# First feed-forwards: gate and up products of steps three to eleven all by Strassen's scheme

## The chip, the cores and the metric

One core of one Trainium2 chip runs the whole program. The time is that of one execution on the device in microseconds (us). The engines are named as in the profile: PE is TensorE (matmuls), DVE is VectorE, ACT is ScalarE, POOL is GpSimd, SP is SyncE, which issues the DMA loads.

## What is computed

A residual stream x of 512 tokens by 1024 features (float32) goes through two stacks of two layers. Each layer of the first stack is a feed-forward, a token mixing and a second feed-forward; each layer of the second is a mixing and a feed-forward with a causal convolution. The change touches the four feed-forwards of the first stack ("first feed-forwards"), cut to what matters:

```python
def rmsnorm(x, g):                       # x / sqrt(mean(x * x) + eps) * g
def swiglu(h, w_gate, w_up, w_down):     # silu(h @ w_gate) * (h @ w_up), then @ w_down
...
for l in range(DEPTH):                   # DEPTH 2, D_MODEL 1024, D_FF 2816
    f = swiglu(rmsnorm(x, ffn1_pre_g[l]), ffn1_w_gate[l], ffn1_w_up[l], ffn1_w_down[l])
    x = x + FFN_RESIDUAL_WEIGHT * rmsnorm(f, ffn1_post_g[l])
    m = token_mixing(...)
    x = x + rmsnorm(m, mix_post_g[l])
    f = swiglu(rmsnorm(x, ffn2_pre_g[l]), ffn2_w_gate[l], ffn2_w_up[l], ffn2_w_down[l])
    x = x + FFN_RESIDUAL_WEIGHT * rmsnorm(f, ffn2_post_g[l])
```

## The kernel before

**Numbers.** Float32 products are made of three matmuls on rounded halves: every weight and activation is split into a high part (a rounding copy by ScalarE) and a low part (the rest, a subtraction by VectorE), and TensorE adds high x high, high x low and low x high into one PSUM bank (`part_mm`, lines 698 to 700, and `tile_mm`, 647 to 649).

**Steps and granules.** The gate and up products of a feed-forward have eleven steps (0 to 10 in the code, one to eleven in words). A step makes 256 of the 2816 hidden columns and has four granules of 512 weight rows by 256 columns (512 KB): q = 0, 1 for w_gate into banks 0 to 3, q = 2, 3 for w_up into banks 4 to 7. A plain granule (`pe_up_granule`) is 8 tiles of 3 matmuls with 512 moving columns, so 24. A Strassen granule (`pe_strassen`) works on the 2 x 2 block form of the product in the Winograd variant: seven products in place of eight for each pair of row blocks, so 2 x 7 x 3 = 42 matmuls with 256 moving columns. It needs four sums of weight blocks (`sums_split`, tile wsum, then sumhi and sumlo), four sums of activation blocks (`t_sums`, `t_hi`, `t_lo`), and seven partial results that are put together behind it (`combine`).

**Which steps.** Steps one and two are plain. In the loop over steps three to ten (`FIRST` to `LAST` - 1) the gate granules are plain and the up granules Strassen. Step eleven is plain. Behind it come the w_down products (`pe_out`), in four column pairs of six granules.

**Order.** Each engine has its order written out by hand; semaphores tie them. Tiles raw, whi, wlo, sumhi and sumlo have two slots, q % 2. SP loads the raw weights of a granule when the low part of the granule two before is made (`load_raw`). ScalarE makes the high part when that granule's matmuls are over (`split_hi`, line 632). VectorE makes the sums (1361 to 1366), the low part of the weights (639) and, behind ScalarE's copy of the sums (1150), their low part (1369). TensorE waits for both low parts. VectorE waits for a result of its own by a semaphore (`ch.wait()`).

**VectorE's turn of the loop before** is: sums-and-split block of granule (i, 3); hidden product of the step before (1495), one hidden low part (1396); gate times r into S (1448), which frees banks 0 to 3; plain low parts of (i + 1, 0) and (i + 1, 1); `combine` of the up results (1384 to 1391), release of banks 4 to 7, two products with r (1461); block of (i + 1, 2). r is the inverse root of the mean square of x. ScalarE's turn has the high parts, the sums' copies, one hidden high part (1155) and two silus (1176).

## Time and profile before

| | us |
|---|---|
| median of two runs (3360.22 and 3362.19) | 3361.2 |
| the profiled execution, its span (the page gives no other time of it; the median is 1.7 above) | 3359.5 |
| TensorE busy | 3304.6 |
| VectorE busy | 2065.5 |
| ScalarE busy | 1504.9 |

The span runs from the first to the last instruction. Busy shares are averages over stages that have different limits, so stretches are read one by one. In a timeline row the first number is the start in us from the span's start and the second the duration; where a row stands for several instructions (x2), the duration is that of all. Durations of consecutive instructions of one engine overlap a little, so the distance from start to start is what one costs its queue. The first feed-forward runs from about 25 to 380 us of the span, its step three from 65.3.

### The profile page before, as it was taken

The numbers are of one execution on the slowest core, as the hardware profiler recorded it, in microseconds if no ns is written. First come the engines' busy times: TensorE is split into PE (matmuls) and PEld (weight loads), VectorE is DVE, ScalarE is ACT, GpSimd is POOL, SyncE is SP. The second block draws the span as 40 slices with busy tenths as digits, with TensorE's granted clock in tenths as the row PEclk, the third lists the DMA queues.
The fourth block names the chain that finished last, engine by engine and source line by source line (L and its number), as shares of the span: only waits on it lengthen the run. The fifth ranks groups of instructions, "written<-read, shape, count | busy, mean of one in ns | idle before, by whom it ended". The sixth has DMA issues, their size and how long they took to land.

```text
span 3359.5 us, 56027 instructions
## 1 busy us (share of the span) xinstructions
PE 3304.6 (98%) x22342; PEld 2941.2 (88%) x22342; DVE 2065.5 (61%) x2942; ACT 1504.9 (45%) x2508; POOL 289.8 (9%) x157
## 2 busy tenths in 40 slices
PE   8999999999999999999999999999999999999999
PEld 7887876788889888876788889889999998899998
DVE  6882556678627882556678726746665277476643
ACT  5342445543335342445553334565443254754432
POOL 1000022100000000022100001210000022100000
PEclk9999999999999999999999999999999999999999
DMA  4343321233333332321233332212223322122222
GB/s 120 100 125 102 106 57 57 70 91 98 97 98 88 100 99 92 105 59 55 70 89 99 93 102 76 57 47 78 93 87 96 102 68 55 57 82 91 90 88 88
DMA packets 330747, 287.62 MB, mean 86 GB/s; under 512 B 9697, under 2 KB 326201, under 8 KB 330581
## 3 DMA queue, kind: packets, MB, share of 16 engines
q1 hardware_dynamic: 330117, 284.17, 28.2%
q8 instruction: 121, 1.98, 0.3%
q10 hardware_dynamic: 464, 1.10, 0.1%
q14 instruction: 45, 0.37, 0.0%
HBM read 283.10 MB, written 5.27 MB: 86 GB/s over the span
## 4 chain that ended last, share of the span: by engine, by line
PE 90%; DVE 5%; ACT 3%; DMA 1%; issue 1%; ACTq 0%; SPq 0%; DVEq 0%
PE ps L647 18%; PE ps L648 18%; PE ps L649 18%; PE ps L698 6%; PE ps L700 6%; PE ps L699 6%; PE ps L753 2%; PE ps L2113 2%; PE ps L2115 2%; PE ps L2114 2%; PE ps L1698 1%; PE ps L757 1%; PE ps L1737 1%; PE ps L1722 1%; PE ps L2163 1%
## 5 line engine op out<-in xcount | busy, mean ns | idle before, releaser
L639 DVE TENSOR_TENSOR wlo<-raw,whi 128x1024 fp32r<-128x1024 f32 (+1 forms) x412 | 495.2, 1202 | 753.0 <-ACT whi L632 750.0
L632 ACT ACTIVATE whi<-raw 128x1024 fp32r<-128x1024 f32 (+1 forms) x493 | 511.6, 1040 | 946.7 <-PE ps L649 790.4
L647 PE MATMUL ps<-xhi,whi 128*128 128x512 f32 (+2 forms) x2576 | 864.5, 336 | 2.0 <-DVE wlo L639 2.0
L648 PE MATMUL ps<-xlo,whi 128*128 128x512 f32 (+2 forms) x2576 | 853.1, 331 | 0.0
L649 PE MATMUL ps<-xhi,wlo 128*128 128x512 f32 (+2 forms) x2576 | 850.6, 330 | 0.0
L647 PEld LDWEIGHTS ps<-xhi,whi 128*128 128x128 f32 x2576 | 485.9, 189 | 65.0 <-issue 17.5
L649 PEld LDWEIGHTS ps<-xhi,wlo 128*128 128x128 f32 x2576 | 484.5, 188 | 47.8
L648 PEld LDWEIGHTS ps<-xlo,whi 128*128 128x128 f32 x2576 | 485.6, 188 | 42.0 <-issue 0.5
L647 PE MATMUL ps<-hhi,whi 128*128 128x512 f32 (+2 forms) x1056 | 359.0, 340 | 0.7 <-issue 0.7
L648 PE MATMUL ps<-hlo,whi 128*128 128x512 f32 (+2 forms) x1056 | 358.1, 339 | 0.0
L649 PE MATMUL ps<-hhi,wlo 128*128 128x512 f32 (+2 forms) x1056 | 357.7, 339 | 0.0
L832 POOL TENSOR_TENSOR S<-S 128x512 f32<-128x512 f32 (+5 forms) x58 | 79.6, 1372 | 2236.1 <-ACT S L859 2184.2
L639 POOL TENSOR_TENSOR wlo<-raw,whi 128x1024 fp32r<-128x1024 f32 (+1 forms) x81 | 203.9, 2518 | 739.8 <-ACT whi L632 739.8
L647 PEld LDWEIGHTS ps<-hhi,whi 128*128 128x128 f32 x1056 | 198.9, 188 | 25.7 <-issue 2.5
L649 PEld LDWEIGHTS ps<-hhi,wlo 128*128 128x128 f32 x1056 | 198.5, 188 | 24.4
L648 PEld LDWEIGHTS ps<-hlo,whi 128*128 128x128 f32 x1056 | 198.9, 188 | 22.8
L700 PE MATMUL ps<-xhi,wlo 128*128 128x256 f32 (+2 forms) x544 | 153.0, 281 | 0.0
L1176 ACT ACTIVATE S<-S 128x512 f32<-128x512 f32 (+2 forms) x132 | 82.0, 635 | 156.2 <-DVE S L1448 116.5
L2113 PE MATMUL ps<-xhi,whi 128*128 128x264 f32 x480 | 145.5, 303 | 2.0 <-DVE m_vt L2513 1.1
L1433 DVE SCALAR_TENSOR_TENSOR S<-S,par 128x528 f32<-128x528 f32 (+1 forms) x176 | 126.3, 759 | 23.2 <-ACT S L1142 17.2
L698 PE MATMUL ps<-xhi,whi 128*128 128x256 f32 (+2 forms) x480 | 139.2, 290 | 0.0
L2114 PE MATMUL ps<-xlo,whi 128*128 128x264 f32 x480 | 137.7, 287 | 0.0
(322 smaller groups left out, 6714.9 us busy)
## 6 DMA issues: line engine op xcount, KB each, us to landing
raw<-in_ffn_w_up_dram SPq DMA_DIRECT2D x176, 512.0 KB, 3.7
raw<-in_ffn_w_down_dram SPq DMA_DIRECT2D x120, 512.0 KB, 3.5
raw<-in_w_in_dram SPq DMA_DIRECT2D x94, 512.0 KB, 3.8
raw<-in_ffn_w_gate_dram SPq DMA_DIRECT2D x88, 512.0 KB, 3.8
raw<-in_w_out_dram SPq DMA_DIRECT2D x32, 512.0 KB, 3.4
raw<-in_ffn_w_down_dram SPq DMA_DIRECT2D x24, 256.0 KB, 2.8
tbias_scratch<-rev_scratch SPq DMA_DIRECT2D x1, 3072.0 KB
y<-tbias_scratch SPq DMA_DIRECT2D x6, 512.0 KB, 4.7
```

Of the source, the lines that this page charges most:

```text
L632: act.activation(into[:, 0:n], raw[slot][:, 0:n], ACT.Copy).then_inc(b.s.weights_hi, 1)
L639: eng.tensor_tensor(lo[:, 0:n], raw[slot][:, 0:n], hi[:, 0:n].bitcast(F32), ALU.subtract).then_inc(b.s.weights_split, 1)
L647: pe.matmul(o, wh, hi[:, t0:t0 + w], start=first, stop=False)
L648: pe.matmul(o, wh, lo[:, t0:t0 + w], start=False, stop=False)
L649: ins = pe.matmul(o, wl, hi[:, t0:t0 + w], start=False, stop=last)
L698: pe.matmul(o, wh, hi, start=first, stop=False)
L699: pe.matmul(o, wh, lo, start=False, stop=False)
L700: return pe.matmul(o, wl, hi, start=False, stop=last)
L1176: act.activation(S[2 + o][:, 0:b.T], S[2 + o][:, 0:b.T], ACT.Silu).then_inc(b.s.silu_done, 1)
L1433: ins = dve.scalar_tensor_tensor(out=c_, in0=S[o][:, k:k + b.T], scalar=tap(l, k, 2 * i + o, up), in1=c_, op0=ALU.mult, op1=ALU.add)
L2113: pe.matmul(o, wh, xhi[:, t, t0:t0 + w], start=(t == 0), stop=False)
L2114: pe.matmul(o, wh, xlo[:, t, t0:t0 + w], start=False, stop=False)
```

## The change

- **TensorE**: the loop runs over steps three to eleven (9 turns), and all four granules of a step are Strassen granules. The gate's partial results use banks 0 to 3 and the up results' banks 4 to 7 in the same layout. Signs are arranged differently: the first hidden half of a step comes out negative and is turned back in `silu` and in the hidden splits.
- **VectorE**: four sums-and-split blocks a step. A block has three sums in place of four (one 128x512, two 128x256); the low part of the weights has 768 of 1024 columns, since one block of the four isn't used by itself. `combine` runs for gate and up; its first copy goes to ScalarE (`corner`). Gate times r is one 128x1024 operation, and so is the hidden product. The up results aren't multiplied with r. The hidden low parts of steps two to eleven leave the loop and stand behind it, between the first w_down splits.
- **ScalarE**: high parts of 768 columns, a copy of the sums with each, a corner copy for gate and up. The hidden high parts leave the loop, too.
- **Norm**: since the up results lack r, the w_down result is larger by 1 / r. The norm behind it takes that out, but for eps, so a tile ye with eps / r^2 in 128 shares is made by ScalarE beside the norm of x (`act_pre_norm`) and added by POOL to the sum of squares (`pool_y`), and the logarithm takes no bias there.

The core of the diff:

```diff
-STRASSEN_GRAN = 2 * (LAST - FIRST)
+ROUNDS = LAST - FIRST
+STRASSEN_GRAN = 4 * ROUNDS + 4
+COMBINED = 2 * ROUNDS + 2
 EARLY = UP_ITERS - 1
...
+            if KIND[g] == "F1":
+                act.activation(ye[:, t0:t0 + w], ps[:, sum_bank(g, f"pre {h}"), 0:w], ACT.Copy,
+                               bias=EPS * EPS * D / P, scale=EPS / P).then_inc(e.eps_made, 1)
...
+            if KIND[g] == "F1":
+                pool.wait_ge(e.eps_made, 2 * KIND[:g + 1].count("F1"))
+                pool.wait_ge(e.y_summed, done)
+                add(acc[:, 0:b.T], ye[:, 0:b.T])
...
+                        (0, 0, True, True, w(a, 1), xs(2 * kp, 0)),
+                        (1, 1, True, False, w(a, 3), xs(2 * kp + 1, 0)),
+                        (3, 0, True, False, w(a, 2), ts(3, kp)),
+                        (3, 1, False, True, ws(a, 3), xs(2 * kp + 1, 1)),
+                        (2, 0, True, False, ws(a, 0), ts(2, kp)),
+                        (1, 0, False, True, ws(a, 2), ts(1, kp)),
+                        (2, 1, False, True, ws(a, 1), ts(0, kp))):
+                    ins = part_mm(pe, ps[:, b0 + bank, h * hw:h * hw + hw], *wt, *mv,
+                                  s2 == 0 and a == 0 and first, s2 == 1 and a == 1 and last)
...
-                with pe.Fori(FIRST, LAST) as i:
+                with pe.Fori(0, ROUNDS + 1) as j:
                     for q in range(4):
-                        (pe_up_granule if q < 2 else pe_strassen)(pe, b, l, f, i, q)
-                for q in range(4):
-                    pe_up_granule(pe, b, l, f, LAST, q)
+                        pe_strassen(pe, b, l, f, FIRST + j, q, 4 * j + q + 1)
             pe.wait_ge(b.s.hidden_free, f.ev(l) + 2 * UP_ITERS - 1 + CR)
...
+            def blocks_hi(i, q, count):
+
+                act.wait_ge(b.s.weights_landed[q % 2], 16 * (f.gb2(l) + 2 * i + q // 2) + 16)
+                act.wait_ge(b.s.granules_done, gb + 4 * i + q + 1)
+                act.activation(blocks(whi[q % 2]), blocks(raw[q % 2]), ACT.Copy).then_inc(b.s.weights_hi, 1)
+                sums_hi(count, q)
+
+            def corner(i, up):
+
+
+                act.wait_ge(b.s.granules_done, gb + 4 * i + 2 * up + 2 + CR)
+                act.wait_ge(b.s.hidden_free, f.ev(l) + 2 * i + up + CR)
+                act.activation(S[0][:, SEQ // 2:SEQ], ps[:, 4 * up, 0:SEQ // 2], ACT.Copy).then_inc(b.s.corner_out, 1)
...
-                hi_split(2, 0)
+                blocks_hi(FIRST, 0, 1)
                 t_hi(2, 3)
-                hi_split(2, 1)
+                blocks_hi(FIRST, 1, 2)
                 if g == 0:
                     act_constants(act)
...
+                with act.Fori(0, ROUNDS) as j:
+                    i = FIRST + j
+                    corner(i, 0)
+                    blocks_hi(i, 3, 4 * j + 4)
+                    silu(i, True)
+                    blocks_hi(i + 1, 0, 4 * j + 5)
+                    corner(i, 1)
+                    blocks_hi(i + 1, 1, 4 * j + 6)
+                    blocks_hi(i + 1, 2, 4 * j + 7)
+                corner(LAST, 0)
+                blocks_hi(LAST, 3, STRASSEN_GRAN)
+                silu(LAST, True)
+                for k in range(2, BESIDE_LAST):
                     hidden_hi(k)
-                hi_split(LAST, 2)
-                for k in range(LAST + 6, 2 * LAST):
+                hi_split(LAST + 1, 0)
+                corner(LAST, 1)
+                hi_split(LAST + 1, 1)
+                for k in range(BESIDE_LAST, 16):
                     hidden_hi(k)
-                hi_split(LAST, 3)
-                silu(LAST)
-                hi_split(LAST + 1, 0)
...
+                v = raw[q % 2][:, :].rearrange("p (a x c) -> p a x c", a=2, x=4)
+                w = wsum[:, :].rearrange("p (a j c) -> p a j c", a=2, j=4)
                 dve.wait_ge(b.s.weights_landed[q % 2], 16 * (f.gb2(l) + 2 * i + q // 2) + 16)
-                if q == 3:
-                    dve.wait_ge(b.s.sums_split, count - 1)
-                elif not isinstance(i, int):
-                    dve.wait_ge(b.s.sums_split, count - 1)
-                ch(dve.tensor_tensor(s4[:, 0, :, :], a21, a22, ALU.add))
-                ch(dve.tensor_tensor(s4[:, 2, :, :], a11, a21, ALU.subtract))
+                dve.wait_ge(b.s.sums_split, STRASSEN_GRAN * n + count - 1)
+                ch(dve.tensor_tensor(w[:, :, 0:2, :], v[:, :, 1:3, :], v[:, :, 0:1, :].to_broadcast([P, 2, 2, P]),
+                                     ALU.add))
                 ch.wait()
-                ch(dve.tensor_tensor(s4[:, 1, :, :], s4[:, 0, :, :], a11, ALU.subtract))
+                ch(dve.tensor_tensor(w[:, :, 2, :], w[:, :, 1, :], v[:, :, 1, :], ALU.add))
                 ch.wait()
-                dve.tensor_tensor(s4[:, 3, :, :], a12, s4[:, 1, :, :], ALU.subtract).then_inc(b.s.sums_made, 1)
-                lo_split(i, q)
-                dve.wait_ge(b.s.sums_hi, count)
+                dve.tensor_tensor(w[:, :, 3, :], w[:, :, 2, :], v[:, :, 3, :], ALU.add).then_inc(b.s.sums_made, 1)
+                dve.wait_ge(b.s.weights_hi, gb + 4 * i + q + 1)
+                dve.tensor_tensor(blocks(wlo[q % 2]), blocks(raw[q % 2]), blocks(whi[q % 2]).bitcast(F32),
+                                  ALU.subtract).then_inc(b.s.weights_split, 1)
+                dve.wait_ge(b.s.sums_hi, STRASSEN_GRAN * n + count)
                 dve.tensor_tensor(sumlo[q % 2][:, :], wsum[:, :], sumhi[q % 2][:, :].bitcast(F32),
                                   ALU.subtract).then_inc(b.s.sums_split, 1)
 
-            def combine():
+            def combine(count, up):
...
+                dve.wait_ge(b.s.corner_out, COMBINED * n + count)
+                ch(dve.tensor_tensor(SS[:, 0:d + 2:d + 1, 0:hw], both(1),
+                                     p1.unsqueeze(1).to_broadcast([P, 2, hw]), ALU.add))
                 ch.wait()
-                ch(dve.tensor_tensor(SS[:, 0:5:4, 0:hw], both(5), p1.unsqueeze(1).to_broadcast([P, 2, hw]), ALU.add))
+                ch(dve.tensor_tensor(u, both(2), v2.unsqueeze(1).to_broadcast([P, 2, hw]), ALU.add))
                 ch.wait()
-                ch(dve.tensor_tensor(u, both(6), S[0][:, 0:hw].unsqueeze(1).to_broadcast([P, 2, hw]), ALU.add))
+                ch(dve.tensor_tensor(cross, both(3), u, ALU.add))
+                ch(dve.tensor_tensor(S[d][:, hw:SEQ], ps[:, b0 + 2, hw:SEQ], u[:, 0, :], ALU.add))
                 ch.wait()
-                ch(dve.tensor_tensor(cross, both(7), u, ALU.add))
-                ch(dve.tensor_tensor(S[5][:, hw:2 * hw], ps[:, 6, 0:hw], u[:, 1, :], ALU.add))
-                ch.wait()
 
             def hidden_lo(k):
...
+                two = SS[:, 2:4, 0:SEQ]
+                src = ps[:, 0:4:2, :]
+                if combined is not None:
+                    combine(combined, 0)
+                    src = two
+                dve.tensor_tensor(two, src, r[:, 0:SEQ].unsqueeze(1).to_broadcast([P, 2, SEQ]),
+                                  ALU.mult).then_inc(b.s.gate_in, 2)
                 dve.wait_ge(b.s.gate_in, f.hb(l) + 2 * i + 2)
                 dve.sem_inc(b.s.hidden_free, 1)
...
+            def hidden(i):
+
+                dve.wait_ge(b.s.silu_done, f.hb(l) + 2 * i + 2)
+                dve.tensor_tensor(hf[:, bass.ds(2 * i, 2), 0:SEQ], SS[:, 4:6, 0:SEQ], SS[:, 2:4, 0:SEQ],
+                                  ALU.mult).then_inc(b.s.hidden_done, 2)
...
+            gate(1)
+            t_sums()
+            sums_split(FIRST, 0, 1)
+            t_lo()
+            sums_split(FIRST, 1, 2)
+            plain_up(1)
+            sums_split(FIRST, 2, 3)
+            if g == 0:
...
+                sums_split(i, 3, 4 * j + 4)
                 dve.wait_ge(b.s.hidden_done, f.hb(l) + 2 * i)
-                gate(i)
-
-            start, stop, per = (1, UP_ITERS, 6) if b.conv else (FIRST, LAST - 1, 13)
-            with dve.Fori(start, stop) as i:
-                base, n0 = ch.base, ch.n
-                ch.base = base + (i - start) * per
-                if b.conv:
-                    lo_split(i, 3)
-                    gate(i)
-                else:
-                    step(i)
-                lo_split(i + 1, 0)
-                lo_split(i + 1, 1)
-                up(i)
+                gate(i, 2 * j + 1)
+                sums_split(i + 1, 0, 4 * j + 5)
+                sums_split(i + 1, 1, 4 * j + 6)
+                up(i, 2 * j + 2)
+                sums_split(i + 1, 2, 4 * j + 7)
+                hidden(i)
                 assert ch.n == n0 + per, ch.n - n0
-            ch.base, ch.n = base, n0 + per * (stop - start)
-            if not b.conv:
-                step(LAST - 1)
-                lo_split(LAST, 0)
-                lo_split(LAST, 1)
-                up(LAST - 1)
-                hidden(LAST - 1)
-                for k in range(LAST, LAST + 4):
-                    hidden_lo(k)
-                lo_split(LAST, 2)
-                for k in range(LAST + 4, 2 * LAST - 2):
-                    hidden_lo(k)
-                lo_split(LAST, 3)
-                dve.wait_ge(b.s.hidden_done, f.hb(l) + 2 * LAST)
-                gate(LAST)
-                for k in range(2 * LAST - 2, 2 * LAST):
-                    hidden_lo(k)
-                lo_split(LAST + 1, 0)
-                lo_split(LAST + 1, 1)
-                up(LAST)
-            dve_out(dve, b, g, gb + UP_GRAN, DOWN_Q, ch, 3)
+            ch.base, ch.n = base, n0 + per * ROUNDS
+            sums_split(LAST, 3, STRASSEN_GRAN)
+            dve.wait_ge(b.s.hidden_done, f.hb(l) + 2 * LAST)
+            gate(LAST, COMBINED - 1)
+            for k in range(2, BESIDE_LAST):
+                hidden_lo(k)
...
```

## Rows read from the trace of the kernel before

**Rows 1.** The page: busy shares, the chain, the loads of w_up.
```profile
PE 3304.6 (98%) x22342; PEld 2941.2 (88%) x22342; DVE 2065.5 (61%) x2942; ACT 1504.9 (45%) x2508; POOL 289.8 (9%) x157
...
PE 90%; DVE 5%; ACT 3%; DMA 1%; issue 1%; ACTq 0%; SPq 0%; DVEq 0%
...
raw<-in_ffn_w_up_dram SPq DMA_DIRECT2D x176, 512.0 KB, 3.7
```

**Rows 2.** Stretches: width, busy us (count) of TensorE, loads, VectorE, ScalarE, POOL; clock, DMA, GB/s.
```profile
86.25:97.60 11.35, 11.35 (x50) 9.08 (x49) 9.47 (x16) 3.19 (x3) 0.00 (x0) 1.00 0.34 96
76.29:86.25 9.96, 9.96 (x85) 9.91 (x83) 7.75 (x11) 4.85 (x6) 0.00 (x0) 1.00 0.26 83
97.61:118.93 21.32, 21.32 (x134) 18.95 (x134) 17.43 (x27) 8.04 (x10) 0.00 (x0) 1.00 0.35 98
54.20:65.30 11.10, 11.10 (x50) 9.00 (x49) 9.95 (x11) 7.26 (x8) 0.00 (x0) 1.00 0.27 81
...
65.30:259.10 193.80, 192.56 (x1153) 169.04 (x1152) 157.45 (x236) 77.78 (x97) 1.37 (x3) 1.00 0.38 114
```

**Rows 3.** VectorE in order of time: start, us, line, operation, idle before.
```profile
110.46 0.69 DVE L1386 TENSOR_TENSOR S<-ps,S 128x512 f32<-128x512 f32 x1
111.18 0.69 DVE L1388 TENSOR_TENSOR S<-ps,S 128x512 f32<-128x512 f32 x1
...
113.08 1.30 DVE L1461 TENSOR_TENSOR S<-S,r 128x512 f32<-128x512 f32 x2 [0.15 <-DVE S L1391]
114.62 0.42 DVE L1361 TENSOR_TENSOR wsum<-raw 128x256 f32<-128x256 f32 x1 [0.23 <-DVE S L1461]
114.96 0.42 DVE L1362 TENSOR_TENSOR wsum<-raw 128x256 f32<-128x256 f32 x1
115.41 0.42 DVE L1364 TENSOR_TENSOR wsum<-wsum,raw 128x256 f32<-128x256 f32 x1
115.87 0.42 DVE L1366 TENSOR_TENSOR wsum<-raw,wsum 128x256 f32<-128x256 f32 x1
...
117.42 1.23 DVE L1369 TENSOR_TENSOR sumlo<-wsum,sumhi 128x1024 fp32r<-128x1024 f32 x1
118.68 0.42 DVE L1361 TENSOR_TENSOR wsum<-raw 128x256 f32<-128x256 f32 x1
```

**Rows 4.** One group of one shape: count, busy us, mean ns, idle before.
```profile
L1950 DVE TENSOR_TENSOR m_w<-m_w,m_scan 128x768 f32<-128x768 f32 x6 | 5.7, 958 | 0.2
```

**Rows 5.** ScalarE in order of time.
```profile
103.84 1.23 ACT L1176 ACTIVATE S<-S 128x512 f32<-128x512 f32 x2 [3.18 <-DVE S L1448]
104.98 1.04 ACT L632 ACTIVATE whi<-raw 128x1024 fp32r<-128x1024 f32 x1
...
116.33 1.06 ACT L1150 ACTIVATE sumhi<-wsum 128x1024 fp32r<-128x1024 f32 x1 [1.94 <-DVE wsum L1366]
...
236.40 3.22 ACT L1155 ACTIVATE hhi<-hf 128x512 fp32r<-128x512 f32 x6
```

**Rows 6.** VectorE ahead of the loop.
```profile
56.55 1.28 DVE L1448 TENSOR_TENSOR S<-ps,r 128x512 f32<-128x512 f32 x2
57.98 1.23 DVE L1408 TENSOR_TENSOR tsum<-hf 128x1024 f32<-128x1024 f32 x1 [0.15 <-DVE S L1448]
...
62.66 1.22 DVE L639 TENSOR_TENSOR wlo<-raw,whi 128x1024 fp32r<-128x1024 f32 x1
```

**Rows 7.** TensorE's first product of w_down, in order of time.
```profile
259.10 0.47 PE L647 MATMUL ps<-hhi,whi 128*128 128x512 f32 x1 [0.73 <-issue]
```

**Rows 8.** Stretches at and after short stands of TensorE, columns as in rows 2.
```profile
3345.40:3347.20 1.80, 0.01 (x1) 0.05 (x1) 0.85 (x2) 1.39 (x4) 0.00 (x0) 1.00 0.00 0
3347.40:3351.30 3.90, 3.90 (x20) 3.63 (x19) 2.38 (x4) 2.73 (x6) 0.00 (x0) 0.56 0.10 42
...
2235.50:2248.40 12.90, 12.90 (x56) 10.65 (x54) 1.69 (x2) 4.54 (x12) 2.36 (x1) 0.50 0.12 41
1585.20:1587.00 1.80, 0.12 (x2) 0.13 (x2) 0.94 (x2) 1.39 (x3) 1.31 (x1) 1.00 0.00 0
```

More of the change, by code:

```diff
@@ L1501, in dve_ffn @@
                     ch(dve.memset(S[o][:, 0:2], 0.0))
+                gate(0)
+                lo_split(1, 1)
+                conv_up(0)
+                with dve.Fori(1, UP_ITERS) as i:
+                    base, n0 = ch.base, ch.n
+                    ch.base = base + (i - 1) * 6
+                    lo_split(i, 3)
+                    gate(i)
+                    lo_split(i + 1, 0)
+                    lo_split(i + 1, 1)
+                    conv_up(i)
+                    assert ch.n == n0 + 6, ch.n - n0
@@ new lines, in dve_ffn @@
+            ch.base, ch.n = base, n0 + per * ROUNDS
[4 more added lines that the diff above has]
+                hidden_lo(k)
+            lo_split(LAST + 1, 0)
+            lo_split(LAST + 1, 1)
+            up(LAST, COMBINED)
+            hidden(LAST)
+            for k in range(BESIDE_LAST, 11):
+                hidden_lo(k)
+            lo_split(LAST + 1, 2)
@@ L1557, in dve_out @@
+            for k in range(11, 18):
+                hidden_lo(k)
+            lo_split(LAST + 1, 3)
+            for k in range(18, KF):
+                hidden_lo(k)
+            dve_out(dve, b, g, gb + UP_GRAN, DOWN_Q, ch, 4)
         def dve_out(dve, b, g, gb, qs, ch, first=2):
```

212 lines of the change are left out of this document (95 added, 117 removed).

## The prediction

> **What bounds the kernel now.** I read the page first: TensorE is busy 98% of the span, and the chain that ended last lies on it for 90% [rows 1]. That names the bound of the whole, not of the stage that is changed, so the stretch windows come next. In step three of the first feed-forward its two Strassen granules take 9.96 us and the two plain ones after them 11.35; the next whole step takes 21.32, with TensorE busy in all of it and VectorE busy for 17.43 [rows 2]. The reader is to see two things: a pair of plain granules costs 1.4 us more than a Strassen pair, of which the loop's turn is part (the pair 54.20 to 65.30, outside the loop, takes 11.10); and VectorE already has only 3.9 us to spare of 21.3. So matmuls bound these steps today, and the question is whether they still do.
>
> **What TensorE saves.** Twenty granules of each first feed-forward turn from plain to Strassen: the gates of steps three to eleven (18) and the up products of step eleven (2). That is ten pairs at 11.10 - 9.96 = 1.14, or 11.4 us for each of four feed-forwards, about 46 us in all. A step's matmuls then take 2 x 9.96 = 19.9, with the loop's turn (about 0.2) 20.15. This is all the change can give: 1.4%.
>
> **What VectorE has to do for a step.** I walk its queue by distances from start to start, since they hold the overlap and the waits. One sums-and-split block, from the rows of today's block [rows 3]:
> - The first sum, now 128x512 and with a wait behind it: 0.73, as 110.46 to 111.18.
> - The second sum, 128x256 with a wait: 0.45, as 114.96 to 115.41.
> - From the start of the last sum to the low part of the sums: 1.55 today (115.87 to 117.42). Between them lies the low part of the weights, which shrinks from 1024 to 768 columns: a 128x768 operation takes 958 ns [rows 4], 1024 columns 1.23 us. I give nothing for that. The sums' low part needs ScalarE's copy of them, which starts at 116.33, when the last sum ends, and takes 1.06 [rows 5]: 117.39, and VectorE goes on at 117.42. The copy ends this wait already now; 0.42 + 1.06 and two hand-overs remain 1.55.
> - The low part of the sums: 1.26 ahead of another block (117.42 to 118.68); 1.15 ahead of an operation that doesn't wait for it, the 0.11 being what a wait adds (0.45 against the 0.34 of 114.62 to 114.96).
>
> That is 3.88 for a block, or 3.99. Today a step has two of these blocks (4.06) and two bare splits; the new one has four blocks, three at 3.88 and one at 3.99: 15.6. The combination from its second operation on took 110.46 to 113.08, so 2.62, and is now needed twice; that of the gate has no release of a bank behind it (2.52), but the 128x1024 product with r and its wait and release (1.15 + 0.23, the latter from 56.55 to 57.98 less two products at 0.60 [rows 6]; 0.60 as the third part of the combination, 0.61). The hidden product as one operation: 1.15. Behind the gate ScalarE does two silus (1.14 [rows 5]) before the high part of the next weights, under 1.04, which comes about 0.2 after VectorE's three sums (1.5) and its turn from the gate. Sum: 15.6 + 2.6 + 2.5 + 1.4 + 1.15 + 0.2 = **23.5 us a step**, against 20.15 of matmuls and 21.32 now. The hidden splits that leave the loop (0.6 a step) and the products of the up results with r are taken off in this.
>
> Does any of the waits hide it? In VectorE's order the gate's combination needs granule two of its step, which ended some 5 us before, and the up combination granule four, which ended about 6 us before. A raw buffer is freed at least 7.7 us before it is read again (low part 1.2, a block 3.9, the up combination 2.6), and a load of 512 KB lands in 3.7 [rows 1]. So nothing stretches VectorE's 23.5, and nothing shortens it: TensorE stands about 3.0 us before the first gate granule of each step and 0.5 elsewhere.
>
> **The ends of the loop.** Step three's gates now need the low parts of the x sums too. VectorE gets to its block for the first granule at 62.66, where the split stood [rows 6], ends it at 66.5, and the four low parts at 1.14 take it to 71.1. The plain gates started at 65.3 [rows 2], so TensorE stands 5.8 us. Then the second block (75.0), the products of step two (76.4), the third block (80.3), the fourth, held 0.5 by ScalarE's corner copy, which waits for the second granule until 81.2 (84.8). Eight periods of 23.5 follow: step eleven's last block ends at 272.8. Its last granule takes 5.0, but the first w_down weights come behind ScalarE's silus (until +5.0), six high parts at 0.53 (8.1), the high part of the weights, 1.04 (9.2), and VectorE's low part, 1.2 (10.4) [rows 5, 3]. w_down's products start at 283.3; today at 259.1 [rows 7]. **+24.2 us.** The hidden low parts that follow keep ahead: the last of them, near 299, is wanted at 283.3 + 20 x 1.39 = 311, with 1.39 as six products of 0.232 (11.10 / 48 [rows 2]). Four stages of one code and one size make 97; ScalarE's and VectorE's constants, 4 us of work in the first stage alone, now stand in the way there and cost about 1. Together 98.
>
> What is costed at nothing: the added copy of the mean square (two of 128x256 on ScalarE, each under the 0.53 of a 128x512 copy [rows 5], ahead of the silu of step one), hidden by the two plain steps, in whose pair VectorE is busy for 9.95 of 11.10 and ScalarE for 7.26 [rows 2]; without that cover 1 us a stage. The added POOL sum (one 128x512, by VectorE's 0.69 an estimated 0.7 to 2) goes in behind the fifth, with a whole w_down column of 30 us before it is read; without cover that much a stage. SP issues the same loads.
>
> **The clock.** The rows show that a short stand costs more than itself. After 1.8 us with TensorE almost idle the granted clock was 0.56 over the next 3.9 us, in the second stack it once was 0.50 (1.2 GHz) for 12.9; another stand of 1.8 left it at 1.00 [rows 8]. The stands of 5.8 and 5.4 at the ends are longer than any of these. I take both as followed by 4 us at 1.2 GHz, so 2 us lost each: 4 x 4 = 15 or 16. Those inside the loop probably lower it too, but 2 us more on the gate granules vanish in TensorE's 3.4 us of slack. In the Trainium skill, "TensorE: Matmul & The Clock Gate", section "HAM oscillation — how this bites in real kernels", a gap that recurs with every tile drops the clock every time; by that alone each step would lose some, and whether this shows in the time hangs on the slack.
>
> **Sum.** 3359.5 of the profiled span + 98 + 15 = 3472.5; the median of the two runs is 1.7 above the span, so **3474 us**, 3.4% slower. A difference under 2% (67 us) is about what a measurement can't tell from none.
>
> **Rivals.**
> - *VectorE keeps pace, so not slower.* Its 30 operations without any wait would need 13.3 for the four blocks (0.60 + 0.34 + 0.34 + 0.89 + 1.15 each), 4.3 for the combinations and 2.3 for the products: 19.9, just the matmuls' 19.9. It decides at a period of 20.5 (24.2 / 8 below mine). At 20.15 a stage loses 24.2 - 26.8 = -2.6: 3351 us; with both stands at the ends gone as well, 3361 - 50 = 3311. Against it: each of today's blocks shows the waits. 0.06.
> - *The last 0.3 us of the block isn't ScalarE's copy,* so that the shorter weights part counts: 22.3 a step, 14.6 a stage, 3361 + 58 + 16 = 3435. 0.08.
> - *Waits for own results cost nothing.* The trace has 0.34 between two sums without and 0.45 with a wait [rows 3]. If the fourteen of them in a step cost nothing, it would take 23.5 - 14 x 0.11 = 21.9, a stage 11.4, the kernel 3361 + 46 + 15 = 3422. 0.04. The Trainium skill, "VectorE: DVE Perf Modes", section "The DRAIN you can't avoid", says this: a semaphore behind each operation came out no dearer than one behind the last. By that rule the trace does not agree here.
> - *The clock stays low after each stand in the loop,* as it did for 12.9 us. Then the two gate granules take 17 instead of 10, ScalarE's high parts wait for them, and a step takes about 27.7; at every second step 47 us a stage, at each 64: 3550 to 3620. A few longer stretches only: 3500. For it: the stands in the loop are longer than the 1.8 that it takes. Against: the other row has it back within 3.9 us [rows 8]. 0.12.
> - *The change does less than it says,* a loop with plain granules left in it: 3361. The diff leaves none. 0.02.
>
> **Numbers.** The forecast has 0.68, and its own range is 3445 to 3500 (blocks 0.15 longer, an eighth of their waits on top, give a step of 24.1 and 3494; no clock loss 3458). The range for 8 in 10 is 3424 to 3530, which takes in the second rival and the mild form of the fourth. Slower by over 2%: 0.68 + 0.12 + most of 0.08 = 0.86; within 2%: 0.13; faster by over 2%, which all of TensorE's saving can't reach: 0.01.
>
> **What would show it.** Step period in the first feed-forwards 23.5 and VectorE busy in over 95% of it; TensorE waiting for the low parts of the sums, about 3 us before each first gate granule; stands of 5 to 6 us before step three and before w_down. A period of 20.2, with VectorE idle somewhere in it, would refute me, and so would low parts of sums that start right behind the weights' low part.

## The result, and the profile after

The changed kernel takes 3477.3 us (median of two runs, 3476.4 to 3478.2) against 3361.2: a ratio of 1.036, 95% interval 1.034 to 1.038, so 3.6% slower. The forecast was 3474.

Two lines of the page after, the engines' busy time and the chain that ended last; then the three longest of TensorE's waits (who waited, for what: us in total, times, longest).

```profile
PE 3304.2 (95%) x23782; PEld 3021.3 (87%) x23782; DVE 2257.8 (65%) x3162; ACT 1569.6 (45%) x2668; POOL 294.3 (8%) x161
...
PE 70%; DVE 16%; issue 7%; ACT 6%; DVEq 1%; DMA 0%; ACTq 0%
```

```profile
PE ps L708 <- DVE sumlo L1396: 80.6, 44, 2.9
PE ps L708 <- DVE tlo L1456: 23.9, 4, 6.0
PE ps L657 <- issue: 18.9, 4, 5.1
```

Against [rows 1], TensorE's share of the last chain falls from 90% to 70%, and VectorE's rises from 5% to 16%, ScalarE's from 3% to 6%. TensorE's busy time is the same 3304 us, although it has less to multiply: a busy TensorE at a low clock counts as busy, and the mean granted clock fell from 0.996 to 0.980. What is new are the three waits, 123 us together: for the low parts of the sums of weights, in the loop; for those of the sums of x, once ahead of each loop; and for w_down's first block ("issue"), once behind it.

The period of a step is read from the product with r, which stands once in each step on VectorE (its first and last start), then the stretches, columns as in [rows 2]: the whole loop with its ends, one step, the first plain stand, and 6 us around a stand in the loop.

```profile
L1498 DVE TENSOR_TENSOR S<-S,r x9: 1225/1226/1227, 91.2 to 281.3; 128x1024 f32<-128x1024 f32 x9
```

```profile
65.30:290.00 224.70, 196.46 (x1525) 193.65 (x1524) 201.97 (x284) 91.23 (x128) 0.57 (x3) 0.93 0.31 98
108.51:132.27 23.76, 20.92 (x165) 20.72 (x164) 21.54 (x32) 7.97 (x10) 0.00 (x0) 0.93 0.28 89
70.00:76.00 6.00, 2.37 (x11) 2.38 (x12) 5.71 (x7) 1.27 (x3) 0.00 (x0) 0.51 0.06 20
120.00:126.00 6.00, 5.39 (x32) 5.39 (x33) 5.50 (x9) 1.28 (x2) 0.00 (x0) 0.72 0.55 173
```

Eight periods take 281.3 - 91.2 = 190.1, so 23.76 each, against 21.32 in [rows 2]. In one of them VectorE is busy for 21.54, and what is left of the 23.76 is waits inside its own queue. TensorE is busy for 20.9, part of it at a lower clock. One step of VectorE, whole:

```profile
108.51 0.68 DVE L1386 TENSOR_TENSOR wsum<-raw 128x512 f32<-128x512 f32 x1
109.23 0.43 DVE L1389 TENSOR_TENSOR wsum<-wsum,raw 128x256 f32<-128x256 f32 x1
109.69 0.42 DVE L1391 TENSOR_TENSOR wsum<-wsum,raw 128x256 f32<-128x256 f32 x1
110.04 0.95 DVE L1393 TENSOR_TENSOR wlo<-raw,whi 128x768 fp32r<-128x768 f32 x1
111.25 1.23 DVE L1396 TENSOR_TENSOR wlo<-wsum,sumhi 128x1024 fp32r<-128x1024 f32 x1 [0.26 <-ACT sumhi L1168]
112.39 0.69 DVE L1416 TENSOR_TENSOR S<-ps,S 128x512 f32<-128x512 f32 x1
...
114.96 1.23 DVE L1498 TENSOR_TENSOR S<-S,r 128x1024 f32<-128x1024 f32 x1
116.52 0.69 DVE L1386 TENSOR_TENSOR wsum<-raw 128x512 f32<-128x512 f32 x1 [0.34 <-DVE S L1498]
...
120.58 0.69 DVE L1386 TENSOR_TENSOR wsum<-raw 128x512 f32<-128x512 f32 x1
...
124.46 0.68 DVE L1416 TENSOR_TENSOR S<-ps,S 128x512 f32<-128x512 f32 x1
...
127.25 0.69 DVE L1386 TENSOR_TENSOR wsum<-raw 128x512 f32<-128x512 f32 x1 [0.33 <-DVE S L1422]
...
131.13 1.22 DVE L1511 TENSOR_TENSOR hf<-S 128x1024 f32 x1
132.27 0.69 DVE L1386 TENSOR_TENSOR wsum<-raw 128x512 f32<-128x512 f32 x1
```

ScalarE's copy of the first of these sums, and TensorE where its waits end: a gate granule in the loop, and w_down's first product in the first feed-forward.

```profile
110.15 1.06 ACT L1168 ACTIVATE sumhi<-wsum 128x1024 fp32r<-128x1024 f32 x1 [1.90 <-DVE wsum L1391]
```

```profile
120.61 0.38 PE L708 MATMUL ps<-xhi,whi 128*128 128x256 f32 x1 [2.84 <-DVE sumlo L1396]
...
289.18 0.77 PE L657 MATMUL ps<-hhi,whi 128*128 128x512 f32 x1 [4.37 <-issue]
```

The copy takes 110.15 to 111.21, and VectorE goes on at 111.25 with the low part of the sums. TensorE's products wait for that low part.

Where the difference lies, by stages: from step two's gate to w_down's first product a feed-forward took 202.55, 201.66, 201.68 and 201.71 us before; after, 230.32 (58.86 to 289.18), 231.05, 230.30 and 230.89. That is 115.0 of the spans' 116.9.

### The profile page after: what moved, and what is told of

The parts are those of the page before. It is cut to its first block, busy times and chain, and to the rows that moved or that the text cites. A ratio compares the mean times of both kernels' runs of the same rounds, so it can differ in the third digit from the quotient of the medians.

```text
span 3476.4 us, 60029 instructions
## 1 busy us (share of the span) xinstructions
PE 3304.2 (95%) x23782; PEld 3021.3 (87%) x23782; DVE 2257.8 (65%) x3162; ACT 1569.6 (45%) x2668; POOL 294.3 (8%) x161
## 4 chain that ended last, share of the span: by engine, by line
PE 70%; DVE 16%; issue 7%; ACT 6%; DVEq 1%; DMA 0%; ACTq 0%
PE ps L657 14%; PE ps L658 14%; PE ps L659 13%; PE ps L708 5%; PE ps L710 5%; PE ps L709 5%; ACT sumhi L1168 4%; DVE wsum L1386 3%; PE ps L763 2%; PE ps L2173 2%; DVE wsum L1389 2%; DVE wsum L1391 2%; PE ps L2175 1%; PE ps L2174 1%; DVE sumlo L1396 1%
## 5 line engine op out<-in xcount | busy, mean ns | idle before, releaser
L645 DVE TENSOR_TENSOR wlo<-raw,whi 128x1024 fp32r<-128x1024 f32 (+1 forms) x268 | 318.6, 1190 | 611.4 <-ACT whi L638 607.9
L638 ACT ACTIVATE whi<-raw 128x1024 fp32r<-128x1024 f32 (+1 forms) x349 | 359.3, 1032 | 657.8 <-PE ps L659 563.5
L657 PE MATMUL ps<-xhi,whi 128*128 128x264 f32 (+2 forms) x1936 | 612.2, 316 | 0.0
L658 PE MATMUL ps<-xlo,whi 128*128 128x264 f32 (+2 forms) x1936 | 600.0, 310 | 0.0
L659 PE MATMUL ps<-xhi,wlo 128*128 128x264 f32 (+2 forms) x1936 | 598.8, 309 | 0.0
L659 PEld LDWEIGHTS ps<-xhi,wlo 128*128 128x128 f32 x1936 | 364.1, 188 | 20.4
L708 PE MATMUL ps<-xhi,whi 128*128 128x256 f32 (+2 forms) x800 | 236.6, 296 | 104.5 <-DVE sumlo L1396 80.6
L708 PE MATMUL ps<-thi,sumhi 128*128 128x256 f32 x864 | 251.3, 291 | 0.0
L709 PE MATMUL ps<-tlo,sumhi 128*128 128x256 f32 x864 | 250.7, 290 | 0.0
L709 PE MATMUL ps<-xlo,whi 128*128 128x256 f32 (+2 forms) x800 | 228.7, 286 | 0.0
L1168 ACT ACTIVATE sumhi<-wsum 128x1024 fp32r<-128x1024 f32 x144 | 152.6, 1060 | 163.1 <-DVE wsum L1391 160.9
```

Source lines behind the costliest of these rows:

```text
L638: act.activation(into[:, 0:n], raw[slot][:, 0:n], ACT.Copy).then_inc(b.s.weights_hi, 1)
L645: eng.tensor_tensor(lo[:, 0:n], raw[slot][:, 0:n], hi[:, 0:n].bitcast(F32), ALU.subtract).then_inc(b.s.weights_split, 1)
L657: pe.matmul(o, wh, hi[:, t0:t0 + w], start=first, stop=False)
L658: pe.matmul(o, wh, lo[:, t0:t0 + w], start=False, stop=False)
L659: ins = pe.matmul(o, wl, hi[:, t0:t0 + w], start=False, stop=last)
L708: pe.matmul(o, wh, hi, start=first, stop=False)
```

## The experiments

All were run beside the kernel before, whose medians were 3355.7 to 3356.4 on those chips. Edits are against the changed kernel.

**1. Half copies.** ScalarE copies the sums in two halves, the first as soon as VectorE's first sum is there.

```diff
-act.activation(sumhi[q % 2][:, :], wsum[:, :], ACT.Copy).then_inc(b.s.sums_hi, 1)
+act.wait_ge(b.s.sums_begun, STRASSEN_GRAN * n + count)
+act.activation(half(sumhi[q % 2], 0), half(wsum, 0), ACT.Copy)
+act.wait_ge(b.s.sums_made, STRASSEN_GRAN * n + count)
+act.activation(half(sumhi[q % 2], 1), half(wsum, 1), ACT.Copy).then_inc(b.s.sums_hi, 1)
```

> ScalarE copies the sums in two halves; the first half (the 128x512 sum) starts as soon as VectorE has made it, so only a 128x512 copy (0.62 us) is left behind the last sum instead of 1.06. Theory (VectorE's queue bounds the step, and in each block it waits 0.26 to 0.3 us for ScalarE's copy): the wait goes, a block falls from 3.88 to about 3.58, the period from 23.77 to 22.6, the time by 4 x (8 x 1.2 + 1) = 42 to about 3435 us. Rival (the copy is not what holds VectorE there, the low part of the weights or its own pace is): block 3.88, period 23.8, time 3477. Rival (TensorE's clock or its matmuls bound the step): no change either.

Measured: 3443.6 us, ratio 1.026 (1.024 to 1.028), 34 us less than the changed kernel. A block of VectorE, in order of time, and the product with r over the loop:

```profile
140.28 0.69 DVE L1392 TENSOR_TENSOR wsum<-raw 128x512 f32<-128x512 f32 x1
...
141.81 0.95 DVE L1399 TENSOR_TENSOR wlo<-raw,whi 128x768 fp32r<-128x768 f32 x1
142.68 1.22 DVE L1402 TENSOR_TENSOR wlo<-wsum,sumhi 128x1024 fp32r<-128x1024 f32 x1
```

```profile
L1504 DVE TENSOR_TENSOR S<-S,r x9: 1224/1226/1227, 89.5 to 271.7; 128x1024 f32<-128x1024 f32 x9
```

The low part of the sums now starts 0.87 behind that of the weights, with no wait between; a block takes 3.53 (140.28 to 143.81) in place of 3.88. The period is (271.7 - 89.5) / 8 = 22.78; 0.98 x 32 periods = 31 of the 34 us. So the copy did end every block. The expected 3435 was 8 too low: six of the eight periods are 22.63, the third and the sixth 23.2 to 23.3, and there a block waits for ScalarE's copy of the weights. The rows put this down to TensorE's clock. After the third period's stand of TensorE it is at 0.57, after one of the same 2.41 us in a short period at 1.00 (columns as in [rows 2]):

```profile
140.31:144.31 4.00, 4.00 (x21) 4.00 (x22) 3.93 (x6) 1.26 (x2) 0.00 (x0) 0.57 0.49 134
186.20:190.20 4.00, 4.00 (x33) 4.00 (x34) 3.93 (x6) 1.26 (x2) 0.00 (x0) 1.00 0.47 131
```

The corner copy starts 11.8 us after the first gate product (140.31 to 152.11), where it is 10.3 with the clock at 1.00 (117.67 to 127.97), and the copy of the weights stands behind it, so that VectorE's low part of them waits 0.38 for it (153.26). Two such periods of 0.6 more in each feed-forward make 5 of the 8 us, if the other three are like the first. In experiment 7, too, the two long periods of the first loop (23.13 and 23.30) are the two with a low clock (0.63 over the 4 us from 117.57, 0.59 from 208.60). No run kept the clock up there, so the cause is read from rows.

**2. A smaller low part of the weights**, of one block of three.

```diff
-dve.tensor_tensor(blocks(wlo[q % 2]), blocks(raw[q % 2]), blocks(whi[q % 2]).bitcast(F32),
+dve.tensor_tensor(blocks(wlo[q % 2])[:, :, 0:P], blocks(raw[q % 2])[:, :, 0:P],
+                  blocks(whi[q % 2]).bitcast(F32)[:, :, 0:P],
```

> The low part of the weights is made for one block in three only (128x256 instead of 128x768); the other two keep old values, so part of the product is left out. It takes 0.55 us of VectorE's work out of every block, 2.2 us a step. Theory: in three of four blocks VectorE then waits for ScalarE's copy of the sums for that much longer, the block stays at 3.88 and the time near 3475 us (at most 0.2 a step, 6 us in all, less). Rival (VectorE's busy time is what counts, and the wait is a shadow of it): period 21.6, time about 3400.

Measured: 3475.3 us, 1.035 (1.033 to 1.037). Two operations of VectorE and the product with r:

```profile
118.95 0.43 DVE L1391 TENSOR_TENSOR wsum<-wsum,raw 128x256 f32<-128x256 f32 x1
119.29 0.42 DVE L1393 TENSOR_TENSOR wlo<-raw,whi 128x256 fp32r<-128x256 f32 x1
120.50 1.22 DVE L1397 TENSOR_TENSOR wlo<-wsum,sumhi 128x1024 fp32r<-128x1024 f32 x1 [0.79 <-ACT sumhi L1168]
```

```profile
L1499 DVE TENSOR_TENSOR S<-S,r x9: 1224/1225/1227, 88.4 to 278.4; 128x1024 f32<-128x1024 f32 x9
```

The operation is 0.53 shorter and the wait behind it 0.53 longer (0.79 for 0.26): 118.95 to 120.50 is 1.55, as in the block of the kernel before (115.87 to 117.42 in [rows 3]). The period is 23.75. Work of VectorE that lies under a copy of ScalarE is free, and taking it away gives nothing.

**3. Plain gates,** everything else of the change kept.

```diff
-    pe_strassen(pe, b, l, f, FIRST + j, q, 4 * j + q + 1)
+    if q < 2:
+        pe_up_granule(pe, b, l, f, FIRST + j, q)
+    else:
+        pe_strassen(pe, b, l, f, FIRST + j, q, 2 * j + q - 1)
```

> Only the gate half of the change is undone: gate granules of steps three to eleven are plain again, the up granules of steps three to eleven stay Strassen, the up results stay without r, the hidden splits stay behind the loop. VectorE has two blocks (3.9), two bare low parts (1.2), one combination (2.8), the gate product (1.4) and the hidden product (1.15) for a step, about 15.5 us, so TensorE bounds it. Theory: period 21.3 as in the kernel before, no stand before step three, the stand before w_down small; time 3361 less four Strassen pairs of step eleven (4 x 1.1) = 3356, plus up to 10 where the new order ahead of w_down holds it: 3355 to 3370. Rival (the cost lies in the splits moved behind the loop or in the norm's new parts): it stays above 3390.

Measured: 3347.1 us, 0.997 (0.996 to 0.998): faster than the kernel before. One step, columns as in [rows 2]:

```profile
102.85:123.86 21.01, 21.01 (x134) 18.90 (x133) 14.30 (x20) 7.25 (x9) 0.00 (x0) 1.00 0.35 101
```

VectorE's busy time falls from 17.43 to 14.30 and TensorE is never late. The whole loss is the gates' Strassen scheme; the rest of the change (fewer products with r, wider operations, hidden splits out of the loop, Strassen up products in step eleven) gains 0.3%. That is below the expected 3355 to 3370: a step of the same 134 matmuls takes 21.01 where the kernel before takes 21.32, and no run here isolates why.

**4. Two products on POOL** (gate by r, and hidden), with ScalarE's Silu moved behind the next weights' copy.

```diff
+pool.wait_ge(b.s.hidden_free, f.ev(l) + 2 * i + 1 + CR)
+pool.tensor_tensor(two, two, r[:, 0:SEQ].unsqueeze(1).to_broadcast([P, 2, SEQ]),
+                   ALU.mult).then_inc(b.s.gate_in, 2)
```

> The product of the gate results with r and the hidden product go from VectorE to POOL, which is idle in the loop (two 128x1024 operations, about 2.5 us each there); the high part of the next weights goes ahead of the silu on ScalarE. Theory (VectorE's queue is the bound): VectorE is rid of 1.14 and of 1.4 of 1.56, and of the 0.1 behind the silu: period about 21.1, TensorE 20.15, time 3477 - 4 x 8 x 2.6 = about 3393. Rival (a bound elsewhere): unchanged near 3477. Rival (POOL's operations slow VectorE's, as both read the same memory at once): the period falls by less than 1.5, VectorE's operations beside POOL's take longer than 0.69 and 1.22.

Measured: 3532.6 us, 1.053 (1.051 to 1.055). It missed by 140 us and had the wrong sign. POOL's two products, and VectorE beside the first of them:

```profile
166.88 2.39 POOL L849 TENSOR_TENSOR S<-S,r 128x1024 f32<-128x1024 f32 x1 [10.39 <-DVEq L1511]
179.72 2.41 POOL L853 TENSOR_TENSOR hf<-S 128x1024 f32<-128x1024 f32 x1 [10.45 <-DVEq L1521]
```

```profile
167.00 2.82 DVE L1398 TENSOR_TENSOR wsum<-raw 128x512 f32<-128x512 f32 x1 [0.33 <-DVE S L1434]
```

The first sum takes 2.82 in place of 0.69. It starts 0.12 behind POOL's product, and ends at 169.82, 0.55 after POOL's end at 169.27: by these times VectorE stood still until POOL was nearly done, and then did its work. So each product taken off VectorE saved 1.15 and cost 2.13. The period was 25.66, 1.9 over the changed kernel's, twice 2.13 - 1.15, which leaves nothing visible for the order of Silu and copy.

**5. The ends reordered,** the loop untouched: two sums of x into VectorE's idle time ahead of step two's gate, w_down's first splits ahead of the hidden splits.

```diff
-                silu(LAST, True)
-                for k in range(2, BESIDE_LAST):
-                    hidden_hi(k)
                 hi_split(LAST + 1, 0)
+                silu(LAST, True)
+                for k in range(2, 4):
+                    hidden_hi(k)
...
+            t_sums(0)
             lo_split(1, 3)
```

> The changed kernel with its two ends reordered and the loop untouched: the first two sums of x move ahead of VectorE's last plain split of step two, into the 2.09 us in which it stood idle (ahead of 57.72), and the first two splits of w_down move ahead of the splits of the hidden rows on ScalarE and VectorE. My theory: in the stretch from step two's gate to w_down's first product VectorE's queue sets the end, so what is taken out of it before the loop is saved (2 x 1.15 - 0.25 = 2.1 us), and TensorE's stand before w_down (4.4 to 5.1 us) is nothing but the place of the first split of w_down behind six hidden splits, so it goes entirely; with the clock that such a stand costs (1 to 2 us) that is 7 to 8.5 us per stage, 28 to 34 in all: 3447 us, 3440 to 3455. The period in the loop stays at 23.77. Rival (a stand at the end is only moved: the hidden splits, now later, hold w_down's later rows): only the first end counts, 8 to 10 us: 3467. Rival (the stands before the loop and behind it do not matter, the loop takes back what the start gives): 3473 or more.

Measured: 3445.5 us, 1.026 (1.025 to 1.028). TensorE's waits:

```profile
PE ps L708 <- DVE sumlo L1398: 81.5, 45, 2.9
PE ps L708 <- DVE tlo L1460: 15.0, 4, 3.8
```

The stand before step three is 3.8 in place of 6.0, that before w_down is left in one feed-forward of four (2.9), and the waits in the loop are as they were (81.5 for 80.6), with the period at 23.76 but for one of 24.44. In that one alone the clock was low behind TensorE's stand, though the one before 119.47 is of the same 2.84 us (columns as in [rows 2]):

```profile
119.47:123.47 4.00, 4.00 (x34) 4.00 (x35) 3.68 (x6) 1.06 (x1) 0.00 (x0) 1.00 0.45 130
238.28:242.28 4.00, 4.00 (x18) 4.00 (x19) 3.68 (x6) 1.06 (x1) 0.00 (x0) 0.50 0.44 136
```

The ends gave what the queue said, 32 us, none of which the loop took back.

**6. Filler products,** which serve nothing, over the two stands at the ends (46 and 44 matmuls of 128x256).

```diff
+fill(7, 46)
 with pe.Fori(0, ROUNDS + 1) as j:
...
+if not b.conv:
+    fill(0, 44)
```

> The changed kernel with matmuls that serve nothing (128x256, 46 ahead of the loop into a bank that is still free, 44 ahead of w_down into another) where TensorE stands for 5 to 6 us, so that it is busy through both stands; the loop and its stands of 2 to 3 us are as before. My theory: each of these two stands costs more than itself only by the clock, which was granted at 0.5 behind it for 2 to 4 us, so that the stage begins its work 1 to 2 us late at each; VectorE sets the period, so what is won ahead of the loop is not won at its end, and only the clock behind the w_down stand counts fully: -4 to -12 us in all, 3469 us (3464 to 3475), the period 23.77 as before, the granted clock 0.99 in place of 0.98. Rival (the clock is what lengthened the changed kernel: the low stretches every second step of the loop come from the same cause and vanish too): more than 20 us less, 3450 or below.

Measured: 3466.4 us, 1.033 (1.031 to 1.035), 10 to 11 us less (by the ratios and by the medians). The stretch of the first stand:

```profile
70.00:76.00 6.00, 5.52 (x46) 5.32 (x46) 5.46 (x9) 2.83 (x9) 0.57 (x3) 1.00 0.26 74
```

The clock is 1.00 there in place of 0.51. The period stays 23.76. So the clock behind the stands at the ends costs 10 to 11 us in all. About 5 of it is the first stand's, since each feed-forward is 1.2 to 1.3 shorter up to w_down's first product (229.07 for 230.32 in the first); the expectation had given that stand nothing. In the changed kernel's loop the clock falls in every step from the one at 120.61 on, not in every second, and costs nothing: the seven periods with a fall take 23.75 to 23.77, the first one, without, 23.78.

**7. Ends and half copies together.** The edits of 1 and 5.

> Both remedies for the changed kernel together: the ends reordered, and ScalarE's copy of the sums of the weights in two halves, the first behind the first sum (3443.6 us alone). My theory (two separate terms in VectorE's queue, one in every block of the loop, one at the ends): they add, 3443.6 - 28 to 34 = 3412 (3405 to 3420), which is still 1.5% over the kernel before, since the period stays at 22.63 to 22.85 against its 21.3. Rival (the ends' gain is shared with the shorter blocks, since the stands before the loop and behind it are the same waits seen twice): 3425 or more. No version that keeps Strassen gates in all nine steps comes below 3400.

Measured: 3415.9 us, 1.018 (1.017 to 1.020), 4 to 6 us above the sum of both. The two terms are separate but for that, and what is left is the period, 22.78.

**8. Strassen gates in every second step,** with half copies.

```diff
-with pe.Fori(0, ROUNDS + 1) as j:
-    for q in range(4):
-        pe_strassen(pe, b, l, f, FIRST + j, q, 4 * j + q + 1)
+with pe.Fori(0, ROUNDS // 2) as j:
+    i = FIRST + 2 * j
+    for q in range(4):
+        if q < 2:
+            pe_up_granule(pe, b, l, f, i, q)
+        else:
+            pe_strassen(pe, b, l, f, i, q, 6 * j + q - 1)
+    for q in range(4):
+        pe_strassen(pe, b, l, f, i + 1, q, 6 * j + q + 3)
```

> Strassen gates in every second step only (steps four, six, eight and ten of the plan; the five others take plain gates as in the run with plain gates, 3347.1 us), up products by Strassen's scheme throughout, copies of the sums in halves. What is computed is whole. My theory: TensorE and VectorE each have their queue, and the longer sets the period over a pair of steps. VectorE: one step of 22.63 (measured with half copies) and one of about 16 busy (14.3 busy in 21.0 with plain gates, and its waits) = 39; TensorE: 21.0 + 19.85 = 40.85, since a gate by Strassen's scheme takes 8 of 64 groups of products fewer. So TensorE sets it, the saving of 1.15 us per Strassen gate arrives whole, and 4 stages x 4 gates x 1.15 = 18 us are saved against 3347: 3329 us, 3325 to 3337, about 0.9% under the kernel before. Rival (VectorE's block holds TensorE up within the step, whatever the mean over two steps, since blocks are made one ahead only): no gain in the Strassen step, or a stand of up to 2.8 us in each, 3347 to 3385. Rival (Strassen's gates themselves cost TensorE more than their matmuls say, as by the start of a wait): 3347 with VectorE idle.

Measured: 3358.9 us, 1.001 (1.000 to 1.002): in the range of the rival that a block holds TensorE up within the step. It does, but not through VectorE's queue. The end of a Strassen gate on VectorE, ScalarE beside it, and TensorE's product that waited:

```profile
147.03 1.23 DVE L1520 TENSOR_TENSOR S<-S,r 128x1024 f32<-128x1024 f32 x1
150.43 2.46 DVE L646 TENSOR_TENSOR wlo<-raw,whi 128x1024 fp32r<-128x1024 f32 x2 [2.17 <-ACT whi L639]
```

```profile
148.29 1.15 ACT L1224 ACTIVATE S<-S 128x512 f32<-128x512 f32 x2 [5.09 <-DVE S L1520]
149.35 1.04 ACT L639 ACTIVATE whi<-raw 128x1024 fp32r<-128x1024 f32 x1
```

```profile
151.78 0.49 PE L658 MATMUL ps<-xhi,whi 128*128 128x512 f32 x1 [1.60 <-DVE wlo L646]
```

VectorE stands idle for 2.17 in the very place where TensorE loses 1.60. Neither queue is full: ScalarE's copy of the next weights is queued behind two Silus, and these wait for VectorE's product.

**9. The copy ahead of Silu.** One exchange in 8.

```diff
-                    silu(i + 1, True)
                     hi_split(i + 2, 0)
+                    silu(i + 1, True)
```

> The kernel with Strassen gates in every second step and half copies (3358.9 us), with one exchange on ScalarE: behind a Strassen gate the copy of the next step's first gate block comes ahead of the two Silu operations, not behind them. What is computed is whole. My theory: the run before it lost its gain in one place, a stand of TensorE of 1.6 us before the first plain gate granule of each pair (16 times, 25.2 us), since that block's copy on ScalarE (149.35) stood behind Silu, which waits for the gate product (147.03), though its buffer was free earlier; with the exchange the copy is made by 148, VectorE's low part follows at 148.2 right behind the gate product, and the stand shrinks to under 0.4. The pair then takes 41.4 to 41.9 in place of 43.01: 3359 - 16 x 1.1 to 1.6 = 3333 to 3341 us, 0.45 to 0.7% under the kernel before. Rival (the stand is VectorE's, whose queue over the pair is full, and only shifts to another block): 3352 or more, with waits for sums in place of waits for the plain block.

Measured: 3334.6 us, 0.994 (0.992 to 0.995): 0.64% faster than the kernel before, the fastest version. One pair of steps, and the place of the exchange:

```profile
103.81:144.98 41.17, 41.11 (x302) 38.81 (x302) 35.68 (x49) 17.04 (x27) 0.00 (x0) 1.00 0.35 102
```

```profile
143.21 1.06 ACT L639 ACTIVATE whi<-raw 128x1024 fp32r<-128x1024 f32 x1 [2.05 <-PE ps L711]
146.24 1.16 ACT L1224 ACTIVATE S<-S 128x512 f32<-128x512 f32 x2 [1.97 <-DVE S L1520]
```

The copy runs 3 us before the Silu that it had waited behind. The pair takes 41.17 in place of 43.01, with TensorE busy for 41.11. A plain-gate step is 21.01 (experiment 3), so the Strassen step is 20.16. Some 0.3 of that lies between three matmuls that start at 137.62, 137.96 and 138.17, where the others of that shape are 0.12 apart.

**10. The same with whole copies.**

> The same kernel with ScalarE's copies of the sums whole, as in the changed kernel, in place of halves. My theory: VectorE's queue over a pair is 6 x 0.3 = 1.8 us longer, 40 to 41 in place of 38 to 39 beside TensorE's 41.4, so that next to nothing comes of it, while with Strassen gates in all steps the same 0.3 cost 34 us: 3333 to 3348, and not over 5 us above the run with half copies. Rival (a term on VectorE counts whatever engine bounds the pair): 16 x 1.8 = 29 us above it, 3362 or more.

Measured: 3341.8 us, 0.996 (0.995 to 0.998), 7 us above 9, where 5 was my limit and 29 the rival's. Columns as in [rows 2], and TensorE's wait in the loops:

```profile
106.31:148.02 41.71, 41.37 (x302) 38.86 (x302) 35.93 (x48) 16.35 (x21) 0.00 (x0) 1.00 0.34 101
```

```profile
PE ps L708 <- DVE sumlo L1412: 5.0, 16, 0.3
```

The 1.8 us that the expectation adds to VectorE's queue come out as 0.54 a pair. A term's price hangs on whose queue is full: 0.3 a block cost 31 us where VectorE set the period, and 7 to 9 us where TensorE nearly did.

## Why the prediction was right, point by point

**The bound moved to VectorE: right.** Period 23.76 forecast at 23.5. The "over 95% busy" that I said would show it did not: VectorE is busy for 21.54 of 23.76, 91%. The rest is its waits for ScalarE's copy (four of 0.16 to 0.26), for two releases and for its own results; a queue can set the period without being busy.

**The terms.** Block 3.88 and 3.99 forecast; 3.88, 4.06, 3.88 and 3.88 measured (the 4.06 with the silu delay in it, forecast 4.19). Gate's combination 2.52: 112.39 to 114.96, 2.57. Hidden product 1.15: 1.14. Mis-sized were the two steps behind a released bank: the gate product with its release 1.38 against 1.56 (114.96 to 116.52), the up combination 2.62 against 2.79 (124.46 to 127.25). I took the releases from places where a product or a sum of x followed; here a block follows, and its first sum starts 0.33 to 0.34 behind the last result. These 0.35, with the 0.05 of the gate's combination and less the 0.13 of the silu, are the whole miss of 0.26.

**The last 0.3 of a block is ScalarE's copy: right,** shown from both sides by experiments 1 and 2. The rival that said 3435 without it is refuted by 2.

**TensorE's saving: right in size,** 20.15 a step forecast, 20.16 in experiment 9, where it is the bound. TensorE's stand before the first gate granule, forecast at 3.0, is 2.84 once and 2.12 to 2.15 in the six steps after that: part of the slack goes into products at the lower clock.

**The ends.** Before step three 5.8 forecast, 6.0 measured; before w_down 5.4 against 4.4 to 5.1. From step two's gate to w_down a feed-forward was forecast 24.2 longer, and 2 for the clock behind the first stand; it was 28.75 longer, and the period's 8 x 0.26 is nearly all the rest. Experiment 5 shows that queue order makes them: the one before w_down goes in three of four, the one before step three shrinks to 3.8.

**The clock: mechanism right, size too large.** 15 to 16 us forecast; the filler gave 10 to 11 back. I had 4 us at the lower clock behind each stand. The row 70.00:76.00 ends 2.4 us after TensorE's first product, and all of that is at 0.51; the clock was back some 3.3 us after it (0.59 over 73.64 to 77.60, 1.00 from there on). In the loop it falls too, to 0.58 over the 4 us behind the stand of 2.84, also some 3.3 us of it, and the period does not move. So the rival of 3550 to 3620 had the fall right; what failed was that the clock stays low. The cost hangs on the slack: the same fall added 0.6 to a period in experiment 1, where VectorE's period is 1.1 shorter, and one of 6.0 us (238.28 to 244.28) added 0.7 in experiment 5. The Trainium skill, "TensorE: Matmul & The Clock Gate", section "HAM oscillation — how this bites in real kernels", says that a recurring gap drops the clock each time; the changed kernel's trace agrees from 120.61 on, experiment 5 does not, where the clock stayed at 1.00 behind five recurring stands of 2.84.

**Own waits cost nothing: refuted** by the rows; no run took waits away. Two 128x256 operations stand 0.46 apart with a wait (109.23 to 109.69) and 0.35 without (109.69 to 110.04), all through the loop. The Trainium skill, "VectorE: DVE Perf Modes", section "The DRAIN you can't avoid", has a semaphore behind each of eight operations cost nothing; here the measurement decides.

**What met by chance.** The first feed-forward began 2.3 us later, and 5.2 us were lost between the stages; in the second stack the 12.9 us at the lower clock [rows 8] were absent, which gave back 5.5. With the 115.0 that is the 117. The period's 0.26 too few over 32 periods, 8 us, and the clock's 4 to 5 too many largely cancel: the 3 us between forecast and result are closer than the terms were. That is luck. The forecast also took a difference under 2% for one that can't be told from none; the intervals here reach 0.1 to 0.2% to either side.

**Open.** It stays open why the clock falls behind one stand and not behind another of the same length. No other order on ScalarE was tried against the 0.6 in experiment 1, nor a share of Strassen gates between half and all.

## What to carry to other kernels

Before work is taken off the bound engine, walk the queue of the engine that pays for it, from start to start with its waits and the other engines' copies in it: 3.9 us of spare VectorE were gone after one block, and TensorE's 1.14 a gate with them. If a saving costs another engine too much in every step, take it in as many steps as that engine can serve: against the run with plain gates (3347.1 us), Strassen gates in four of the nine steps gave 0.4% with half copies (with whole copies 0.1%, within the intervals), and in all nine they cost 3.9%. The rest of the 0.64% is the change without its gates. And where two engines are idle at once, look at the third one's queue for an operation that waits ahead of one that needn't.

## What the runs showed of the hardware that I had not expected

- **POOL stops VectorE.** Beside a POOL product of 128x1024 (2.39) a VectorE sum of two SBUF operands took 2.82 in place of 0.69, and 2.81 beside the one at 179.72. It is in the changed kernel too, in another stage. POOL there, and VectorE's operations beside it:

```profile
458.93 2.60 POOL L645 TENSOR_TENSOR wlo<-raw,whi 128x1024 fp32r<-128x1024 f32 x1 [5.63 <-ACT whi L638]
...
580.70 2.38 POOL L645 TENSOR_TENSOR wlo<-raw,whi 128x1024 fp32r<-128x1024 f32 x1 [6.07 <-ACT whi L638]
```

```profile
459.46 0.42 DVE L2030 TENSOR_TENSOR m_w<-ps,y 128x256 f32<-128x256 f32 x1
...
581.63 1.74 DVE L2004 TENSOR_TENSOR m_w<-m_w,later 128x256 f32<-128x256 f32 x1 [1.43 <-ACT m_w L1902]
```

  With one operand from PSUM, 459.46 runs in its 0.42 inside POOL's operation. With two from SBUF, 581.63 takes 1.74 where the same line takes 0.42 at 622.12, and ends 0.29 after POOL (583.08). The Trainium skill, "SBUF — State Buffer", section "Who interferes with whom", says that a VectorE instruction with two SBUF inputs contends with a GpSimd instruction that reads SBUF, and that such contention is an exclusive lock; both traces agree, and I had not weighed it when I wrote 3393.
- **Handing over between ScalarE and VectorE** took 0.03 to 0.04: the sum's last operation ends at 110.11 and the copy starts at 110.15; that ends at 111.21 and VectorE goes on at 111.25.
- **The length of a stand did not decide the clock.** In the changed kernel it fell behind the stand of 2.84 us (0.72 over 120 to 126, around the first product at 120.61) and behind the six of 2.12 to 2.15 (0.60 to 0.68 over 4 us each). In experiment 5 five stands of 2.84 left it at 1.00 and the sixth did not; in experiment 1 three of 2.41 left it and two did not. Behind the changed kernel's 1.67 us that ended at 96.84 it is 1.00:

```profile
96.84:102.00 5.16, 5.16 (x43) 5.16 (x44) 4.80 (x7) 1.06 (x1) 0.00 (x0) 1.00 0.55 177
```
